# Moving the routing step of a mixture-of-experts loop behind the next expert's first product

## The reference

```python
def swiglu(t, w_up, w_down):
    gate, up = split_cols(t @ w_up, (w_down.shape[0], w_down.shape[0]))
    return (jax.nn.silu(gate) * up) @ w_down
...
_, idx = lax.top_k(jnp.where(expert_mask, choice, -jnp.inf), TOP_K)
w = jnp.take_along_axis(s, idx, axis=1)
w = ROUTED_SCALE * w / jnp.sum(w, axis=-1, keepdims=True)
routed = routed_experts(u, idx, w, w_exp_up, w_exp_down)
```

## Time and profile before

| | us |
|---|---|
| median of 3 runs | 1267.52 (1266.24 to 1271.38) |
| the profiled execution | 1268.87 |
| its span | 1267.0 |
| TensorE (PE) busy in the span | 1168.9 (92%) |
| VectorE (DVE) busy | 918.3 (72%) |
| ScalarE (ACT) busy | 724.0 (57%) |
| GpSimd (POOL) busy | 238.0 (19%) |

### The profile page before, as it was taken

How to read it: one execution, slowest core, us unless ns; L and a number is a source line. 1 busy time by engine, 2 the same in 40 slices (tenths; PEclk the granted TensorE clock), 3 DMA queues, 4 the chain that set the end, 5 groups by cost and what they waited for, 6 DMA issues and landing times.

```text
span 1267.0 us, 17831 instructions
## 1 busy us (share of the span) xinstructions
PE 1168.9 (92%) x5911; PEld 883.1 (70%) x5911; DVE 918.3 (72%) x1343; ACT 724.0 (57%) x926; POOL 238.0 (19%) x146
## 2 busy tenths in 40 slices
PE   4999998999999899898999999999999999999993
PEld 3699987766677788565777666667666666666662
DVE  4576477544433693667999999889889888988882
ACT  7443333334333322425778777777777777777772
POOL 1000000000000000001343342333333332333331
PEclk9999998999999999899999999999999999999998
DMA  6312231212121323727999999999999999999992
GB/s 215 125 58 93 83 112 47 75 59 66 33 67 64 120 100 100 286 76 265 345 353 349 359 365 358 352 347 347 345 342 353 351 343 350 341 345 346 345 291 35
DMA packets 133357, 285.29 MB, mean 225 GB/s; under 512 B 11876, under 2 KB 34424, under 8 KB 133316
## 3 DMA queue, kind: packets, MB, share of 16 engines
q1 hardware_dynamic: 118580, 250.88, 56.0%
q0 software_dynamic: 14736, 33.87, 11.6%
HBM read 272.11 MB, written 29.38 MB: 238 GB/s over the span
## 4 chain that ended last, share of the span: by engine, by line
PE 46%; DMA 31%; DVE 9%; ACT 7%; issue 4%; SPq 1%; DVEq 0%; POOL 0%; POOLq 0%; ACTq 0%
PE bank L1370 36%; DMA arena<-in_w_exp_up_dram 16%; DMA arena<-in_w_exp_down_dram 12%; ACT split L521 5%; DVE split L1258 4%; PE bank L1538 2%; PE bank L1565 2%; DMA arena<-u_rows,arena 2%; PE bank L1449 1%; ACT arena L521 1%; PE bank L1682 1%; PE bank L1550 1%; PE bank L1701 1%; DMA arena<-in_x_dram 1%; DVE arena L944 0%
## 5 line engine op out<-in xcount | busy, mean ns | idle before, releaser
L1258 DVE TENSOR_TENSOR split<-arena,split 128x2048 fp32r<-128x2048 f32 x192 | 438.9, 2287 | 70.1 <-ACT split L521 68.8
L521 ACT ACTIVATE split<-arena 128x2048 fp32r<-128x2048 f32 x192 | 366.9, 1917 | 93.5 <-DMA arena<-in_w_exp_up_dram 76.0
L1370 PE MATMUL bank<-split,gatheredT 128*96 128x512 f32 x1536 | 374.2, 399 | 7.2 <-DVE gatheredT L1265 3.0
L1370 PEld LDWEIGHTS bank<-split,gatheredT 128*96 128x96 f32 x1536 | 244.6, 163 | 112.2 <-issue 5.8
L1370 PE MATMUL bank<-split,hidT 128*96 128x512 f32 x768 | 191.9, 398 | 1.5 <-ACT arena L521 1.5
L474 POOL DMA_INDIRECT arena<-u_rows,arena x64 | 128.4, 2007 | 251.7 <-DVE arena L1274 194.1
L1370 PEld LDWEIGHTS bank<-split,hidT 128*96 128x96 f32 x768 | 119.1, 162 | 47.0 <-issue 1.6
L482 POOL DMA_INDIRECT out_dram<-arena x64 | 101.7, 1589 | 257.7 <-ACT arena L521 180.1
L1370 PE MATMUL bank<-hT_high,front_split 128*128 128x512 f32 x448 | 143.9, 403 | 0.8 <-DVE hT_low L852 0.8
L521 ACT ACTIVATE arena<-bank 96x512 f32<-96x512 f32 (+4 forms) x217 | 107.7, 532 | 57.5 <-PE bank L1370 29.2
L1370 PEld LDWEIGHTS bank<-hT_high,front_split 128*128 128x128 f32 x448 | 81.4, 189 | 28.1 <-issue 11.5
(11 more groups left out here) (237 smaller groups left out, 1346.1 us busy)
## 6 DMA issues: line engine op xcount, KB each, us to landing
arena<-in_w_exp_up_dram SPq DMA_DIRECT2D x128, 1024.0 KB
arena<-in_w_exp_down_dram SPq DMA_DIRECT2D x64, 1024.0 KB
arena<-in_w_in_dram SPq DMA_DIRECT2D x14, 1024.0 KB, 5.5
arena<-in_w_in_dram SPq DMA_DIRECT2D x10, 768.0 KB, 4.5
arena<-in_w_branches_dram SPq DMA_DIRECT2D x4, 1024.0 KB, 5.0
arena<-in_w_out_dram SPq DMA_DIRECT2D x4, 1024.0 KB, 4.9
arena<-in_x_dram SPq DMA_DIRECT2D x4, 512.0 KB, 5.4
arena<-in_w_mem_kv_dram SPq DMA_DIRECT2D x2, 1024.0 KB, 5.2
```

The costliest lines, as they stand in the source:

```text
L521: return nc.scalar.activation(o, i, ACT.Copy, **kw)
L1258: v.tensor_tensor(both[:, 1], raw[q % RAW], both[:, 0].bitcast(F32), ALU.subtract).then_inc(low_done, 1)
L1370: ins = mm(bank, left[a], right[b], start=first and q == 0, stop=last and q == 2)
```

## The change

In TensorE's turn, `route(n + 3)` is moved from ahead of `up(n + 1)` to behind `transpose_tokens(n + 2)`. In VectorE's turn, `read_route(n + 3)` and `choose(n + 4)` are moved from between the turn's first two `low` blocks to behind `low_tokens(n + 2)`. No instruction is added or removed, and no semaphore's count is changed.

```diff
                 if blocks > 0:
                     low(q, u + LEAD)
-                if not last or n + 3 < TURN:
-                    read_route(n + 3, m + 3)
-                if not last:
-                    choose(n + 4, m + 4, e + 4)
                 if blocks > 1:
                     low(q + 1, u + (LEAD + 1))
                 if not last or n + 1 < TURN:
                     hidden(n + 1, m + 1)
                 if not last or n + 2 < TURN:
                     low_tokens(n + 2, m + 2)
+                if not last or n + 3 < TURN:
+                    read_route(n + 3, m + 3)
+                if not last:
+                    choose(n + 4, m + 4, e + 4)
                 if blocks > 2:
                     low(q + 2, u + (LEAD + 2))
...
                 last.then_inc(hidT_done, 1)
-                if not last_turn or n + 3 < TURN:
-                    route(n + 3, m + 3, e + 3)
                 if not last_turn or n + 1 < TURN:
                     up(n + 1, m + 1, u + BLOCKS)
                 if not last_turn or n + 2 < TURN:
                     transpose_tokens(n + 2, m + 2, turn + (n + 2) // 2)
+                if not last_turn or n + 3 < TURN:
+                    route(n + 3, m + 3, e + 3)
                 pe.wait_ge(low_done, u + 3)
```

## The result

The changed kernel takes 1409.08 us, the median of four runs (1407.03 to 1412.11). The kernel before takes 1266.88 us, the median of four. The ratio is 1.1117, 95% interval 1.1083 to 1.1152: **slower by 142 us**, in the direction that was forecast and by more than three times the 44 us.

What follows compares the result with a forecast made beforehand. The expert loop was taken as bound by the DMA weight stream, 10.48 us per expert, with TensorE near its limit. A late gather makes turns 11.20 us, 0.72 more, times 61 = 44 us: forecast 1312 us, range 1268 to 1350.

Steps and rivals of the forecast that it cites:

- The weight stream as second limit: Expert loop: weight loads keep the DMA engines busy, share 1.04, setting 10.48 us per expert; share forecast to fall to 0.97.
- w: TensorE's wait for the gather in each turn of the expert loop, forecast at 1.18 us.
- one equation for a steady turn: Expert loop: gather landing set equal to TensorE's need in the next turn, giving wait = (landing time - 5.04) / 2.
- The rule for the form: Gather on GpSimd: TensorE wait below 1.4 us puts VectorE's third block ahead, long form (2.61 us); above, short (0.98 us).
- L = 7.4: Time from the gather's issue to its landing, taken as 7.4 us, between bounds of 4.0 and 9.5 us.
- The clock, put at nothing: TensorE's granted clock, 1.00 before: a lower one from longer waits would add to the full price; no size given.
- the upper case: Gather landing 9.5 us after issue: TensorE wait 2.23 us, turn 12.25 us, +108 us; as a rival, chance 0.16.
- TensorE's own work, 10.02 us: TensorE's work per expert without any wait: 10.48 us per expert less 0.46 us idle.
- the formula: TensorE's gather wait per turn = (landing time - 5.04) / 2, built on 10.02 us of TensorE work per turn.
- The full price: Rival: gather landing stays 9.5 us after issue though turns lengthen; wait 2.23 us, +108 us, 1375 us; chance 0.16.

Runs made afterwards that it cites:

- the third block held back: Changed kernel, with VectorE's third weight block waiting until GpSimd has issued the gather: 1302.36 us, ratio 1.0275.
- the dead matmuls: Changed kernel plus useless fp32 matmuls on TensorE ahead of its gather wait, each turn: two 1376.54 us, three 1332.41 us; kernel before with three: 1329.25 us.
- the 1258.16 us kernel: Kernel before, with only VectorE's routing reads and choose moved behind the turn's second weight block, ahead of hidden: 1258.16 us, ratio 0.9941.

## Why the prediction was right and wrong

- **Direction, and what is late.** Right. The token numbers were forecast 9.97 us into the turn and the gather at 10.89; in the turn from 949.00 the reads end at 958.89, that is 9.89, and the gather begins at 10.82. The gather became the wait, the hidden block's wait went, and TensorE waits neither for `select` nor for a weight block by more than 2 us. A weight load takes 6.9 to 7.7 us to its landing in the median, and none is left in the chain of waits of the loop.
- **The weight stream as second limit.** Right in kind: the DMA share fell, to 0.90 and not only to 0.97.
- **The price: w the same in each turn.** Wrong, and this is the step of the mechanism that failed. I set up one equation for a steady turn and let long and short form "pull towards" a wait of 1.4 us. The rule for the form was right (no wait, long; a wait of over 1.4 us, short), but they don't settle. A long form gives a wait of 3.7 us; this holds VectorE's third block back until just behind the next gather (972.64 against 972.53 in the turn shown), so that this one is short and meets a queue that runs empty, and it lands after 3.7 us. Then there is no wait, the turn is 9.5 us, the next gather runs into a weight block and a fresh load, and is long again. The mean wait is 1.83 us per turn, not 1.18.
- **L = 7.4 as a mean.** Wrong as a picture: the landings lie at 3.7 and at 8.6 us. That the DMA share fell took little off the long ones (8.6 against 8.9 us), since a weight load is issued at the end of the very block that holds the gather up. In the trace of before I had both forms before me and used them as two ends of a range.
- **The clock, put at nothing.** This is the term of the sum that failed. I named it as an addition to the upper case, gave it no price, and left it out of the forecast. It is 77 us by the granted clock and 85 by the sum, out of 142. Without it a turn would be 9.52 + 1.83 = 11.35 us, against the 11.20 that I forecast: that is 9 us in 61 turns, of the 97 by which the forecast missed. The two errors belong together. I had small waits in every turn in mind, but they come as 3.7 us in every other turn, and what stands behind such a wait takes up to 6.84 us and not 3.78. With even waits of 1.1 us at turns of 11.0 (the third block held back) the clock stayed full.
- **TensorE's own work, 10.02 us.** 0.5 us too high. Idle time in a profile of pipelined matmuls is only what is visible between them. With 9.5 in the formula the wait is 0.26 us longer. That the mean wait of 1.83 us led so near to the forecast turn is luck: the base was 0.5 us too high and the wait 0.65 too low.
- **The rivals.** "The full price" at 0.16 came nearest, 1375; its w of 2.23 per turn was too high and its clock had no price, two errors that partly cancel. Its reason, that the long form persists and a weight load is issued just when the gather is, holds for every other gather. The measured 1409 lies outside my range of 1268 to 1350, which left the clock out.
- The method behind it: of a loop in which one instruction has two lengths, and in which each length changes the start of the next turn, I asked for the balance and never followed the sequence of turns.

Shown by experiments are the gather's lateness (119 us by one wait on GpSimd) and the long form (107 us back when it is prevented, a part of which may be the added wait's own doing). The share of the clock, 77 us, is worked out from the granted clock and was not switched by itself; the dead matmuls changed waits, forms and clock together. That weight loads make the rest of the difference between the two landings is read from the order of times.

## What to carry to other kernels

A prefetch that is "just hidden" had two prices here: nothing for the first 2.5 us, and then far more than the lateness, since TensorE's wait of 3.7 us also halved the clock of the work that followed. Before an issue is moved later, look what the engine beside it will be doing at that moment: 2.2 us later into work that left GpSimd alone gained 9 us here; some 4 us later, right ahead of a blocking instruction, lost 142; with that instruction held back 35 were left. And in a pipelined loop follow two or three turns by hand before taking a mean, because a late turn can make the next one early.

## What the runs showed of the hardware

- The instruction of an indirect gather on GpSimd takes 0.98 us when no weight block (`tensor_tensor`, both inputs in SBUF, 2.28 us) is under way on VectorE. If one is, the gather's instruction ends 0.83 to 0.86 us behind the block's end, in 467 of the 469 long gathers of the loops traced: so it takes 1.4 to 3.0 us, by how much of the block was left. The rows above have it: 962.42 against 961.56. Where both start within 0.03 us of each other, it goes either way (five short with the block just ahead, the two others long with it just behind); a block that starts 0.05 us or more behind the gather never lengthened it. Nor do `hidden` and `low_tokens`, which read one input from a bank: 58 gathers of the 1258.16 us kernel begin beside them and take 0.98.
- TensorE's clock fell to its half without any long idle time: with waits of 1.1 and 0.6 us in each turn of 11.6 to 13.1 us it was granted 0.91 over 640 us. With 62 us of waits for VectorE in 600 us, at turns of 11.0, it was granted 1.00.
- A gather of 96 rows lands by what is queued with it. The short form takes 7.0 us with weight loads all the time (the kernel before, DMA share 1.04) and 3.7 in the changed kernel, where the last weight load is 5.7 us old; the long form takes 8.6 us, and 6.3 with half of the weight bytes.
